# One transfer per expert matrix in a two-layer mixture-of-experts encoder: rows of 16 KB in place of two halves with rows of 8 KB

## The reference

```python
def hier_moe(h, w_rg, w_re, w_gate, w_up, w_down):
    ...
    lg = (xt @ w_rg)                                  # 4 groups, the best one is taken
    grp = jnp.argmax(lg, axis=-1)
    ...
    top_v, top_i = lax.top_k(le, TOP_K_INNER)         # 2 of the 8 experts in that group
    ...
    def run(args):
        xe, e_i = args
        hdn = jax.nn.silu(xe @ w_gate[e_i]) * (xe @ w_up[e_i])
        return hdn @ w_down[e_i]
```

## Time and profile before

| | us |
|---|---|
| median of 3 runs | 1806.28 |
| the profiled execution's own time | 1805.69 |
| its span, first to last instruction | 1803.8 |
| TensorE busy in the span | 1589.4 (88%) |
| VectorE, ScalarE, GpSimd busy | 695.3, 435.6, 194.1 |
| bytes moved by DMA | 527.56 MB, a mean of 292 GB/s |
| expert stage of layer 0, first to last expert product | about 411 to 891 |
| expert stage of layer 1 | about 1287 to 1775 |

### The profile page before, as it was taken

One profiled execution on the slowest core, in us unless ns is written; L12 is line 12 of the kernel. 1 busy time (PEld: TensorE's weight loads), 2 busy tenths in 40 slices (PEclk: granted clock), 3 DMA queues, 4 the chain that ended last, 5 costly groups with the idle time before them and its releaser, 6 DMA issues.

```text
span 1803.8 us, 22591 instructions
## 1 busy us (share of the span) xinstructions
PE 1589.4 (88%) x7494; PEld 763.4 (42%) x7494; DVE 695.3 (39%) x1432; ACT 435.6 (24%) x989; POOL 194.1 (11%) x199
## 2 busy tenths in 40 slices
PE   5999998998998998787889999999899988887883
PEld 2455645453333343333345555455333333333331
DVE  1677576352222112222157855743422222222124
ACT  2111567112111112111121016742111221111111
POOL 0000022111111011111000002101111111111010
PEclk9999999989999999999999999999999999999997
DMA  9625533079999999999972355212799999999994
GB/s 362 231 70 202 195 115 110 17 293 398 407 401 407 408 408 404 417 410 417 365 298 93 122 204 208 68 48 101 290 400 407 403 409 406 411 416 404 399 395 180
DMA packets 118493, 527.56 MB, mean 292 GB/s; under 512 B 16529, under 2 KB 22673, under 8 KB 69265
## 3 DMA queue, kind: packets, MB, share of 16 engines
q1 hardware_dynamic: 100944, 491.49, 69.0%
q0 software_dynamic: 12496, 24.51, 4.2%
q10 hardware_dynamic: 4976, 10.55, 1.6%
HBM read 520.99 MB, written 23.86 MB: 302 GB/s over the span
## 4 chain that ended last, share of the span: by engine, by line
PE 56%; DMA 27%; SPq 6%; DVE 5%; issue 3%; ACT 3%; POOL 1%; ACTq 0%; DVEq 0%; POOLq 0%
DMA ring<-in_w_exp_up 20%; PE ps L1015 18%; PE ps L1373 17%; PE ps L1228 6%; SPq L841 5%; PE ps L1371 4%; DMA hT<-in_w_exp_up 3%; PE ps L1170 2%; PE ps L1184 2%; PE ps L1210 2%; PE ps L1041 1%; DMA ring<-in_w_in 1%; ACT arena L1664 1%; DMA yexp_d<-arena,masks 1%; PE ps L1404 1%
## 5 line engine op out<-in xcount | busy, mean ns | idle before, releaser
L1373 PE MATMUL ps<-ring,arena 128*64 128x512 f32 x1952 | 589.1, 603 | 59.2 <-ACT arena L1664 35.0
L1373 PEld LDWEIGHTS ps<-ring,arena 128*64 128x64 f32 x1952 | 184.8, 138 | 273.5 <-issue 260.2
L1015 PE MATMUL ps<-ring,hT 128*128 128x512 f32 (+1 forms) x768 | 255.0, 487 | 1.5 <-DVE z L1804 0.9
L733 DVE TENSOR_TENSOR arena<-ps,arena 64x512 f32<-64x512 f32 (+1 forms) x64 | 44.3, 693 | 488.6 <-ACT arena L1658 418.6
L1658 ACT ACTIVATE arena<-ps 128x512 f32<-128x512 f32 x64 | 38.2, 597 | 778.9 <-PE ps L1373 724.3
L1015 PEld LDWEIGHTS ps<-ring,hT 128*128 128x128 f32 x768 | 144.4, 191 | 101.5 <-issue 91.2
L1373 PE MATMUL ps<-home,arena 128*64 128x512 f32 x320 | 148.6, 619 | 24.2 <-DMA ring<-in_w_exp_up 20.5
L1373 PE MATMUL ps<-hT,arena 128*64 128x512 f32 x336 | 151.5, 605 | 6.9 <-DMA ring<-in_w_exp_up 6.9
L980 POOL DMA_INDIRECT yexp_d<-arena,masks x64 | 59.3, 927 | 850.3 <-DVE arena L743 772.9
L741 DVE TENSOR_TENSOR arena<-ps,gate 64x512 f32<-64x512 f32 (+1 forms) x64 | 43.7, 683 | 266.2 <-PE ps L1373 246.6
L1228 PE MATMUL ps<-ring,hT 128*128 128x512 f32 x256 | 112.5, 595 | 0.0
(11 more groups left out here) (218 smaller groups left out, 1645.2 us busy)
## 6 DMA issues: line engine op xcount, KB each, us to landing
ring<-in_w_exp_up SPq DMA_DIRECT2D x108, 1024.0 KB
ring<-in_w_exp_down SPq DMA_DIRECT2D x88, 1024.0 KB
ring<-in_w_exp_gate SPq DMA_DIRECT2D x62, 1024.0 KB
ring<-in_w_ada SPq DMA_DIRECT2D x24, 2048.0 KB, 11.1
home<-in_w_exp_gate SPq DMA_DIRECT2D x44, 1024.0 KB
work<-in_w_exp_down SPq DMA_DIRECT2D x40, 1024.0 KB
hT<-in_w_exp_gate SPq DMA_DIRECT2D x22, 1024.0 KB
hT<-in_w_exp_up SPq DMA_DIRECT2D x20, 1024.0 KB
```

The costliest lines, as they stand in the source:

```text
L1015: last = pe.matmul(out, lhs(k), rhs(k), start=(k == 0), stop=(k == n - 1))
L1373: last = [pe.matmul(outs[c][HALF * c:HALF * c + HALF, :], lhs(k)[:, 0:HALF], rhs(c, k), start=(k == 0), stop=(k == n - 1), tile_position=( ...
```

## The change

A matrix is brought by one transfer of 2 MB, whose rows are the whole 16 KB of a partition. The two semaphores of each place become one (`place_in`). TensorE waits for whole matrices before the first product of a block and no longer announces halves. SyncE waits once per reload, for the finished product, and then issues the whole transfer.

```diff
-                def load_half(i, e, h):
-                    b, n = BUF[l][i], KD * 512 // 2
-                    sp.dma_start(places[b][:, n * h:n * h + n], flat[i % SPAN][e][:, n * h:n * h + n]).then_inc(half_in[h][b], 16)
+                def load_whole(i, e):
+                    b = BUF[l][i]
+                    sp.dma_start(places[b][:, :], flat[i % SPAN][e]).then_inc(place_in[b], 16)
...
                 for i in range(NBUF):
                     await_first_free(BUF[l][i])
-                    for h in range(2):
-                        load_half(i, i // SPAN, h)
+                    load_whole(i, i // SPAN)
...
                 def expert_unit(it, r, c):
                     b = (0, 1, 6)[c]
-                    sp.wait_ge(down_half if c == 2 else gate_up_half, SPAN * it + (NE * l + r - SPAN + 1))
-                    load_half(SPAN * r + c, SPAN * it + r, 0)
                     sp.wait_ge(filled[b], SPAN * it + (expert_bank(l, b) + r - SPAN + 1))
-                    load_half(SPAN * r + c, SPAN * it + r, 1)
+                    load_whole(SPAN * r + c, SPAN * it + r)
...
-                def pair(w, outs, lhs, rhs, n, arrived, half_used):
+                def pair(w, outs, lhs, rhs, n):
                     for k in range(n):
-                        if k % (n // 2) == 0:
-                            arrived(2 * k // n)
...
-                        if k == n // 2 - 1:
-                            last[1].then_inc(half_used, 1)
...
                     def body(w):
+                        for c in range(2):
+                            place_arrived(q, n, c)
                         pe.wait_ge(drained[3], at(3, e) + 1)
...
                     def body(w):
+                        place_arrived(q, n, 2)
                         pe.wait_ge(drained[2], at(2, e) + 1)
```

More of the change, by code:

```diff
@@ L410, in program @@
         slot_in = [sem(f"slot_in{s}") for s in range(SLOTS)]
-        half_in = [[sem(f"place{i}_half{h}_in") for i in range(NBUF)] for h in range(2)]
-        gate_up_half, down_half = sem("gate_up_half_used"), sem("down_half_used")
+        place_in = [sem(f"place{i}_in") for i in range(NBUF)]
         filled = [sem(f"bank_filled{b}") for b in range(8)]
@@ L1353, in turn_tokens, with place_arrived @@
                         last.then_inc(filled[b], 1)
-                def half_arrived(q, n, c, h):
+                def place_arrived(q, n, c):
                     b = BUF[l][SPAN * (n % SPAN) + c]
-                    pe.wait_ge(half_in[h][b], 32 * q + 16 * (uses_before(l, b) + n // SPAN + 1))
+                    pe.wait_ge(place_in[b], 32 * q + 16 * (uses_before(l, b) + n // SPAN + 1))
                 def weights_of(n, c):
@@ L1381, in gate_up, with body @@
                     weights = [weights_of(n, c) for c in range(2)]
-                    def arrived(h):
+                    def body(w):
                         for c in range(2):
-                            half_arrived(q, n, c, h)
-                    def body(w):
+                            place_arrived(q, n, c)
                         pe.wait_ge(drained[3], at(3, e) + 1)
@@ L1393, in body @@
                         ends = pair(w, [bank_e(0), bank_e(1)], lambda k: xgT[j][:, k, :],
-                                    lambda c, k: weights[c][k], KD, arrived, gate_up_half)
+                                    lambda c, k: weights[c][k], KD)
                         for c in range(2):
@@ L1415, in body @@
                         ends = pair(w, [bank_e(5), bank_e(6)], lambda k: hidT[j][:, k, :],
-                                    lambda c, k: weights[2 * k + c], KE, lambda h: half_arrived(q, n, 2, h), down_half)
+                                    lambda c, k: weights[2 * k + c], KE)
                         for c in range(2):
```

## The result

The changed kernel takes 1808.26 us (median of 20 runs, 1803.48 to 1812.24); the kernel before, in as many runs, 1804.47 us (1799.69 to 1807.28). The ratio is 1.0019, with a 95% interval of 1.0011 to 1.0027: by the ratio the change costs 3.4 us (the two medians lie 3.8 us apart). I had forecast 5.6 us less than before. The time lies inside the stated range, but on the wrong side of no change.

What follows compares the result with a forecast made beforehand. DMA transfers of expert matrices, slower than TensorE's products, were taken to set the pace, with lagging engines setting the end. Terms: -15.0 + 2.5 + 1.5 + 5.4 = -5.6 us, so 1800.7 us predicted, range 1792 to 1815.

Steps and rivals of the forecast that it cites:

- longer rows: Expert reloads in both layers: 16 KB rows save 86 ns per matrix over 87 reloads a layer, 15.0 us in all.
- The price of a packet: Expert-matrix queue q1: 9.6 ns per packet beside its bytes, fitted from stretches of 2 KB and 8 KB rows.
- the lagging engines: DMA engines that finish last and set the stage's end, 5.52 us per matrix; claimed to save 86 ns per matrix too.
- First reload: Start of each layer's reloads: issuing only after the whole product loses 2.5 us in layer 1 and 1.5 in layer 0.
- The end of each stage: Last gate-and-up product of each layer: waiting for the whole up matrix costs 2.7 us, 5.4 us for two layers.
- The sum of the edges: Undivided places at both ends of the expert stages: late first reloads and late last products, 9.4 us together.
- The gather: POOL's gathers beside longer packets: may come 1.2 us later, but are asked for two experts ahead, some 27 us.
- the longer row brings nothing: Rival, expert reloads: 16 KB rows save nothing, the undivided places cost 9.4 us, 1815.7 us; chance 0.25.
- Its threshold: Price per packet in the expert reloads below which the no-gain rival decides: 6.0 ns.
- Gaps in the queue: Rival, behind layer 1's early wide expert: the queue runs dry, up to 5 us more, about 1806; chance 0.17.

Runs made afterwards that it cites:

- e1: The changed kernel with each matrix brought by two transfers with rows of 8 KB, places still undivided: 1.0053 of before, 9.6 us above it.
- e9: The changed kernel, gathers and scatters kept, with gate-and-up products that leave out every other k: 1799.82 us.
- e10: As e1 (rows of 8 KB), gathers and scatters kept, with gate-and-up products that leave out every other k: 1805.30 us.
- s1: No model, only a stream of expert matrices with rows of 4, 8 or 16 KB: 64 matrices took 321.3 us with 8 KB, 316.2 us with 16 KB.
- e7: The changed kernel without gathers and scatters, its gate-and-up products leaving out every other k: 1704.82 us.
- e8: As e1 (rows of 8 KB), without gathers and scatters, its gate-and-up products leaving out every other k: 1719.90 us.
- s4: The s1 stream, 8 and 16 KB rows, beside GpSimd's 32-row transfers: 354.0 and 352.9 us beside reads, 334.1 and 328.1 us beside writes.
- e2: The kernel before, but SyncE reloads a place only when its whole product is finished, then issues both halves: 1.0023 of before, 4.2 us.
- e3: The kernel before, but TensorE waits for both halves of its matrices before a block's first product: 1.0014 of before, 2.5 us.
- e4: The changed kernel with halves only for the first two reloads and the last up matrix of a layer: 0.9992 of before, 1802.15 us.

## Why the prediction was wrong

**The step that failed is the size of the term "longer rows".** It was put at 15.0 us ("The whole of it counts"); in this kernel it is 6 us (e1 against the changed kernel) or 5.5 us (e9, e10). With 5.5 in place of 15.0 the forecast's own sum gives 3.9 us more than before; 3.4 were measured. The price of a packet, 9.6 ns, was right (s1: 422, 429, 410 GB/s), and so was its count: e7 and e8 give 15.1 us. What failed is the sentence that the lagging engines "carry the same packets of q1 and more of q0, so they too save 86 ns per matrix". I had fitted the price in two stretches with q1 alone and carried it into stretches with gathers. There the stream's own packets are longer, and the gain of the longer row falls from 110 to 64 ns per matrix (e7 to e10). In the stream by itself each read row of q0 cost an engine 0.05 us more beside 16 KB rows than beside 8 KB rows (s4). A warning stood in rows that I had read: the late windows, with side traffic, ran at 403 to 409 GB/s, and the 6 us of 8 KB rows alone at 422, the rate that s1 later gave. By the fitted price a row of 4 KB on q0 takes 4 x 37.5 + 9.6 ns = 0.16 us, which is what s4 shows for a written one; a read one took 0.41.

**First reload.** Right: 2.5 and 1.5 us forecast, 4.2 us (2.3 to 6.0) measured (e2). The profile after shows the stand-still in layer 1 and the dip to 0.69 in layer 0.

**The end of each stage.** Right in kind, 5.4 us forecast, 2.5 us (0.9 to 4.3) measured alone (e3). The sum of the edges, 9.4 us, agrees with e1's 9.6 us, and that is partly luck: the two measured alone make 6.7 us, and undoing them at the edges gave back some 5 (e4).

**The gather.** I had it later by 1.2 us and hidden. It came 2.8 us later, so that term was too small, but it is hidden: in the changed kernel the view of TensorE's transposes of the gathered tokens (line 1348) shows no wait for a DMA. Its price on the DMA engines is not hidden, and that is a different thing from its latency.

**The rivals.** The measured 1808.26 us fell to "the longer row brings nothing", which had a chance of 0.25 (1808 to 1817). It had the right sign with the wrong reason (scattered addresses) and was, at 1815.7, 7 us too high; the row does bring something. Its threshold of 6.0 ns per packet holds: the saving in the kernel, 6 us over 2 x 87 x 9 packets, is 3.8 ns. "Gaps in the queue" isn't it: behind the early wide expert the share is 0.97 at 392 GB/s in the window from 1342 to 1347 us and 1.00 or more after it.

```profile
1342.00:1347.00 5.00, 5.00 (x17) 2.00 (x14) 1.38 (x2) 0.00 (x0) 1.02 (x2) 1.00 0.97 392
```

The rule in the Trainium skill's "DMA: Bandwidth & Descriptors", section "Why small descriptors are slow (HBM only)", gave a saving of 5 us, as an estimate. As a price of a packet the stream contradicts it (429 against 422 GB/s is 1.7%, not 0.6%); the kernel came out near it by another mechanism.

## What to carry to other kernels

A price fitted where one queue runs alone holds only there: before it is multiplied, fit it once more in a stretch with the traffic that the change will meet. Halving transfers helps at the edges of a stream, where the queue is empty or the last landing is awaited, and longer rows help in the middle; here even both together (e4) are not shown to beat plain halves. And count the small reads of another queue as what they take from the stream, not as their own bytes: in s4 a read row took 0.41 us of it, where a written row of the same 4 KB took 0.16.

## What the runs showed of the hardware

- A packet of this queue costs some 9.6 ns beside its bytes. That was fitted from rows of 2 and 8 KB and fits 410, 422 and 429 GB/s with rows of 4, 8 and 16 KB to 3 GB/s (s1). The number of transfers for the same rows makes no difference (422 and 422).
- A 4 KB row that is read on the second queue takes 0.41 us from its engine's stream of 8 KB rows and 0.46 us beside 16 KB rows; a row that is written takes 0.16 and 0.15 us (s4 against s1).
- Late in a stage SyncE's issue of a pair of halves took mostly 2 to 10 us with no wait between them (e1), the issue of a whole mostly 0.33 us (6.12 us for the last two, in the changed kernel). What that is worth in the kernel no run tells.
- The gathers and scatters, 16.8 MB of 528, cost 85 us of the time where the transfers set the pace (e10 against e8).
